# Reordering the router's chain in a fused two-layer transformer trunk: broadcast behind the logits, choice by token block, gathered rows by feature halves

## The reference

```
x = x + g_m * y                                   # attention's output
h = rms_norm(x, norm_ff[1]) * (1 + sc_f) + sh_f
logits = h @ router                               # 256 x 8
top_v, top_i = top_k(logits, 2); top_w = softmax(top_v)
for e in range(8):                                # w_in[e]: 1024 x 7168, w_out[e]: 3584 x 1024
    y += gates[:, e:e+1] * ((silu(a) * b) @ w_out[e])     # a, b = split(h @ w_in[e])
x = x + g_f * y; return rms_norm(x, final_norm)
```

## Time and profile before

| | |
|---|---|
| median of 3 runs | 1624.5 us (1624.39 to 1627.12) |
| profiled execution, its own time | 1623.05 us |
| its span (first to last instruction) | 1621.1 us |
| mean granted TensorE clock | 0.986 of 2.4 GHz |
| busy: TensorE, VectorE, ScalarE, GpSimd | 96%, 88%, 67%, 4% |
| read from memory | 499.28 MB, 309 GB/s over the span |

### The profile page before, as it was taken

One profiled execution on the slowest core, in us unless ns is written; L12 is line 12 of the kernel. 1 busy time (PEld: TensorE's weight loads), 2 busy tenths in 40 slices (PEclk: granted clock), 3 DMA queues, 4 the chain that ended last, 5 costly groups with the idle time before them and its releaser, 6 DMA issues.

```text
span 1621.1 us, 22979 instructions
## 1 busy us (share of the span) xinstructions
PE 1556.2 (96%) x7356; PEld 1292.5 (80%) x7356; DVE 1421.8 (88%) x1604; ACT 1085.2 (67%) x1224; POOL 59.7 (4%) x47
## 2 busy tenths in 40 slices
PE   5999998999989998999999999999999999999996
PEld 5788776888869777888888888888888888888884
DVE  6988999788878866989989989989989989999995
ACT  3454445344366647778878878878878778778774
POOL 0212200000000110000000000000000000000000
PEclk9999999999999999999999999999999999999998
DMA  9977777888845424999999999999999999999991
GB/s 333 346 251 268 269 263 247 291 287 306 318 179 208 156 79 152 394 363 349 372 366 341 370 371 336 367 376 337 371 373 333 365 376 341 367 375 344 363 378 76
DMA packets 235114, 500.91 MB, mean 309 GB/s; under 512 B 9744, under 2 KB 40640, under 8 KB 235072
## 3 DMA queue, kind: packets, MB, share of 16 engines
q1 hardware_dynamic: 233904, 500.29, 85.2%
q10 hardware_dynamic: 1168, 0.07, 0.0%
HBM read 499.28 MB, written 1.05 MB: 309 GB/s over the span
## 4 chain that ended last, share of the span: by engine, by line
PE 81%; DVE 9%; DMA 3%; issue 3%; ACT 2%; POOL 1%; SPq 0%; ACTq 0%; DVEq 0%; POOLq 0%
PE ps L500 24%; PE ps L502 24%; PE ps L501 24%; DMA ada<-in_ada_w 2%; DVE acc L1477 2%; DVE w_lo L1458 2%; PE ps L988 2%; PE ps L778 1%; PE ps L780 1%; PE ps L782 1%; DMA raw<-in_ret_w_in 1%; PE ps L1021 1%; PE ps L997 1%; PE ps L1022 0%; PE ps L998 0%
## 5 line engine op out<-in xcount | busy, mean ns | idle before, releaser
L1458 DVE TENSOR_TENSOR w_lo<-raw,w_hi 128x1024 fp32r<-128x1024 f32 x834 | 990.6, 1227 | 67.4 <-ACT w_hi L1088 55.3
L1088 ACT ACTIVATE w_hi<-raw 128x1024 fp32r<-128x1024 f32 x834 | 861.0, 1057 | 214.3 <-PE ps L502 188.3
L500 PE MATMUL ps<-w_hi,RA 128*128 128x512 f32 x1528 | 605.7, 396 | 9.9 <-DVE w_lo L1458 3.5
L502 PE MATMUL ps<-w_hi,RA 128*128 128x512 f32 x1528 | 596.5, 390 | 0.0
L501 PE MATMUL ps<-w_lo,RA 128*128 128x512 f32 x1528 | 595.8, 390 | 0.0
L500 PEld LDWEIGHTS ps<-w_hi,RA 128*128 128x128 f32 x1528 | 287.3, 188 | 69.2 <-DVE w_lo L1458 4.2
L502 PEld LDWEIGHTS ps<-w_hi,RA 128*128 128x128 f32 x1528 | 287.2, 188 | 61.1
L501 PEld LDWEIGHTS ps<-w_lo,RA 128*128 128x128 f32 x1528 | 287.7, 188 | 58.0 <-issue 0.7
L500 PE MATMUL ps<-w_hi,hT_hi 128*128 128x512 f32 x400 | 161.0, 402 | 6.4 <-issue 4.0
L502 PE MATMUL ps<-w_hi,hT_lo 128*128 128x512 f32 x400 | 158.3, 396 | 0.0
L501 PE MATMUL ps<-w_lo,hT_hi 128*128 128x512 f32 x400 | 158.0, 395 | 0.0
(11 more groups left out here) (249 smaller groups left out, 1042.1 us busy)
## 6 DMA issues: line engine op xcount, KB each, us to landing
raw<-in_moe_w_in SPq DMA_DIRECT2D x224, 1024.0 KB
raw<-in_moe_w_out SPq DMA_DIRECT2D x112, 1024.0 KB
ada<-in_ada_w SPq DMA_DIRECT2D x46, 1024.0 KB, 7.3
raw<-in_ff_w_in SPq DMA_DIRECT2D x44, 512.0 KB
raw<-in_ret_w_in SPq DMA_DIRECT2D x16, 1024.0 KB
raw<-in_ff_w_out SPq DMA_DIRECT2D x11, 1024.0 KB
raw<-in_ret_w_in SPq DMA_DIRECT2D x16, 512.0 KB
raw<-in_ret_w_out SPq DMA_DIRECT2D x8, 1024.0 KB
```

The lines of the kernel that those rows point to most:

```text
L500: pe.matmul(out, a_hi, b_hi, start=first, stop=False)
L502: return pe.matmul(out, a_lo, b_hi, start=False, stop=last)
L1088: act.activation(w_hi[:, cn % RING, cols], raw[:, cn % RAW, cols], ACT.Copy).then_inc(hi_done, 1)
L1458: v.tensor_tensor(w_lo[:, cn % RING, cols], raw[:, cn % RAW, cols], w_hi[:, cn % RING, cols].bitcast(f32), ALU.subtract).then_inc(lo_done, 1)
```

## The change

The gate's broadcast leaves its place between the second transposes and the second logits; its two matmuls go behind the logits and behind the counts, one each. The second block's sum of x is made in two column halves, each with its own semaphore count, and the transposes wait for each half. The choice is made by token block, and TensorE's first counts wait for block 0 alone; the subtraction for the softmax goes behind the choice. The gathered features are laid out over two PSUM banks so that each engine modulates two chunks of the first 512 features, then two of the second; `up` waits for each 512 features by itself. All calls of `turn_over` go.

```diff
-            def broadcast_gate(g, dg, bank):
+            def broadcast_gate(g, dg, bank, parts=range(2)):
                 pe.wait_ge(diag_ok, g + 1)
-                for n in range(2):
+                for n in parts:
                     last = pe.matmul(ps[:, bank + n, :], ones[:, :],
                                      dg[:, 4 * n:4 * n + 4, :].rearrange("p c q -> p (c q)"), start=True, stop=True)
-                last.then_inc(gbc_done, 1)
+                if 1 in parts:
+                    last.then_inc(gbc_done, 1)
...
             reduce_ada(2, 6)
-            turn_over(4, 20)
...
             def transpose_raw(b):
-                pe.wait_ge(x_ok, 5 + b)
                 for c in range(KC):
+                    if c % 4 == 0:
+                        pe.wait_ge(x_ok, 5 if b == 0 else 6 + c // 4)
...
             transpose_raw(1)
-            broadcast_gate(3, diag3, 2)
             route(1)
-            turn_over(0, 8)
+            broadcast_gate(3, diag3, 2, (0,))
 
             pe.wait_ge(sel_ok, 1)
             pe.matmul(ps[:, 5, 0:8], before[:, :], sel[:, 0, :], start=True, stop=True)
             pe.matmul(ps[:, 5, 8:16], ones[:, :], sel[:, 0, :], start=True, stop=False)
+            pe.wait_ge(sel_ok, 2)
             pe.matmul(ps[:, 5, 8:16], before[:, :], sel[:, 1, :], start=False, stop=True).then_inc(slot_done, 1)
             pe.matmul(ps[:, 1, 0:8], ones[:, :], sel[:, 0, :], start=True, stop=False)
             pe.matmul(ps[:, 1, 0:8], ones[:, :], sel[:, 1, :], start=False, stop=True).then_inc(cnt_done, 1)
+            broadcast_gate(3, diag3, 2, (1,))
...
-            def up(c, m, bank):
+            def up(c, m, bank, gathered=None):
                 for h in range(2):
+                    if gathered is not None:
+                        pe.wait_ge(hgl_ok, gathered + h + 1)
...
-                turn_over(0, 4)
                 transpose_gathered(NE * p)
-                turn_over(0, 14)
-                pe.wait_ge(hgl_ok, NB * NE * p + 2)
-                up(U_MOE, m0, 0)
+                up(U_MOE, m0, 0, 2 * NE * p)
...
             def gathered_high(ne):
                 act.wait_ge(hgT_done, ne + 1)
-                for c in range(4):
-                    ins = act.activation(hg32[:, c, :], ps[:, 6, c * P:(c + 1) * P], ACT.Identity,
-                                         bias=modc[:, FF1 + SH + c:FF1 + SH + c + 1], scale=scol[:, 4, c:c + 1])
-                ins.then_inc(hg32a_ok, 1)
-                act.wait_ge(hg32a_ok, ne + 1)
-                act.activation(hg_hi[:, 0:4, :], hg32[:, 0:4, :], ACT.Copy).then_inc(hgh_ok, 1)
-                act.wait_ge(hg32b_ok, ne + 1)
-                act.activation(hg_hi[:, 4:8, :], hg32[:, 4:8, :], ACT.Copy).then_inc(hgh_ok, 1)
+                for i in range(2):
+                    for c in range(4 * i, 4 * i + 2):
+                        col = c // 4 * S + c % 2 * P
+                        ins = act.activation(hg32[:, c, :], ps[:, 6, col:col + P], ACT.Identity,
+                                             bias=modc[:, FF1 + SH + c:FF1 + SH + c + 1], scale=scol[:, 4, c:c + 1])
+                    ins.then_inc(hg32a_ok, 1)
+                    act.wait_ge(hg32a_ok, 2 * ne + i + 1)
+                    act.wait_ge(hg32b_ok, 2 * ne + i + 1)
+                    act.activation(hg_hi[:, 4 * i:4 * i + 4, :], hg32[:, 4 * i:4 * i + 4, :],
+                                   ACT.Copy).then_inc(hgh_ok, 1)
...
+                if n == 2 and b == 1:
+                    for k in range(2):
+                        cols = slice(k * TW, (k + 1) * TW)
+                        v.tensor_tensor(x[:, b, cols], x[:, b, cols], tmp[:, b, cols], ALU.add).then_inc(x_ok, 1)
...
             for b in range(NB):
                 dve.wait_ge(rt_done, b + 1)
...
+                steps.link(v.scalar_tensor_tensor(logit[:, b, :], ps[:, 6 + b, 0:NE], stat[:, 6 + b:7 + b], sh_e, ALU.mult,
+                                                  ALU.add))
+                steps.link(v.max(mx[:, b, :], logit[:, b, :]))
+                steps.link(v.max_index(ridx[:, b, :], mx[:, b, :], logit[:, b, :]))
+                steps.link(v.tensor_copy(stat[:, 36 + 2 * b:38 + 2 * b], ridx[:, b, 0:2]))
                 for k2, oh in enumerate((oh1, oh2)):
                     ins = v.tensor_scalar(oh[:, b, :], slot_no[:, 0:NE], stat[:, 36 + 2 * b + k2:37 + 2 * b + k2], None,
                                           ALU.is_equal)
...
+                steps.link(ins)
+                v.tensor_tensor(sel[:, b, :], oh1[:, b, :], oh2[:, b, :], ALU.add).then_inc(sel_ok, 1)
+            v.tensor_tensor(stat[:, 32:34], mx[:, :, 1], mx[:, :, 0], ALU.subtract).then_inc(dm_ok, 1)
             normed_low(1)
```

More of the change, by code:

```diff
@@ L549, in transpose_x @@
                         last.then_inc(xT_done, 1)
-            def turn_over(bank, times):
-                for _ in range(times):
-                    pe.transpose(ps[:, bank, 0:P], ident[:, :], ident[:, :])
-            def broadcast_gate(g, dg, bank):
+            def broadcast_gate(g, dg, bank, parts=range(2)):
                 pe.wait_ge(diag_ok, g + 1)
-                for n in range(2):
+                for n in parts:
                     last = pe.matmul(ps[:, bank + n, :], ones[:, :],
                                      dg[:, 4 * n:4 * n + 4, :].rearrange("p c q -> p (c q)"), start=True, stop=True)
-                last.then_inc(gbc_done, 1)
+                if 1 in parts:
+                    last.then_inc(gbc_done, 1)
             pe.wait_ge(const_ok, 1)
@@ L1004, in transpose_gathered @@
                 for c in range(KC):
-                    last = pe.transpose(ps[:, 6 + c // 4, (c % 4) * P:(c % 4 + 1) * P], ht[:, c * P:(c + 1) * P],
-                                        ident[:, :])
+                    col = c // 4 * S + c % 2 * P
+                    last = pe.transpose(ps[:, 6 + c // 2 % 2, col:col + P], ht[:, c * P:(c + 1) * P], ident[:, :])
                 last.then_inc(hgT_done, 1)
@@ L1028, in step @@
                 pe.wait_ge(eg_ok, n)
-                up(c, me, 0)
+                up(c, me, 0, 2 * ne + 2 if j == ET else None)
                 if j == ET + 1:
@@ L1098, in root_mean_square @@
                 if 0 < n < 4:
-                    act.wait_ge(x_ok, NB * (n - 1) + b + 1)
+                    act.wait_ge(x_ok, NB * (n - 1) + b + 1 + (n == 3 and b == 1))
                 if n == 4 and b == 0:
@@ L1543, in add_gated @@
                 steps.link(ins)
-                v.tensor_tensor(x[:, b, :], x[:, b, :], tmp[:, b, :], ALU.add).then_inc(x_ok, 1)
+                if n == 2 and b == 1:
+                    for k in range(2):
+                        cols = slice(k * TW, (k + 1) * TW)
+                        v.tensor_tensor(x[:, b, cols], x[:, b, cols], tmp[:, b, cols], ALU.add).then_inc(x_ok, 1)
+                else:
+                    v.tensor_tensor(x[:, b, :], x[:, b, :], tmp[:, b, :], ALU.add).then_inc(x_ok, 1)
             dve.wait_ge(vecT_done, 1)
@@ L1866, in _ @@
                                           ALU.is_equal)
-            steps.link(ins)
-            v.tensor_tensor(sel, oh1, oh2, ALU.add).then_inc(sel_ok, 1)
+                steps.link(ins)
+                v.tensor_tensor(sel[:, b, :], oh1[:, b, :], oh2[:, b, :], ALU.add).then_inc(sel_ok, 1)
+            v.tensor_tensor(stat[:, 32:34], mx[:, :, 1], mx[:, :, 0], ALU.subtract).then_inc(dm_ok, 1)
             normed_low(1)
@@ L1911, in gathered_low @@
                 dve.wait_ge(hgT_done, ne + 1)
[L1912 to L1915, removed]
+                for i in range(2):
+                    for c in range(4 * i + 2, 4 * i + 4):
+                        col = c // 4 * S + c % 2 * P
+                        ins = v.tensor_scalar(hg32[:, c, :], ps[:, 7, col:col + P], scol[:, 4, c:c + 1],
+                                              modc[:, FF1 + SH + c:FF1 + SH + c + 1], ALU.mult, ALU.add)
+                    ins.then_inc(hg32b_ok, 1)
                 for i in range(2):
```

2 lines of the change are left out of this document (removed).

## The result

The changed kernel takes 1627.85 us (median of 20 runs, 1625.85 to 1631.54) against 1624.6 us of 20 runs of the kernel before: ratio 1.0022, 95% interval 1.0016 to 1.0028, about 3.6 us slower. The profiled execution of the changed kernel, the only one of this kernel whose trace is read here, was one of its longest, 1631.41 us with a span of 1629.7. So its times are read as distances inside a stage and not as places in the span.

What follows compares the result with a forecast made beforehand. TensorE, 81% of the chain and never idle in the expert loops, was taken as the bound, so only the first `up` could move: -1.0 -1.4 +0.4 +0 +0.5 = -1.5 us, from 1624.5 to 1623.0, range 1620.5 to 1626.3.

Steps and rivals of the forecast that it cites:

- part 1, the logits: Second block's logits in the router: start at 606.3 us instead of 608.57, end at 608.2.
- Part 2, ScalarE becomes the late one: Behind the late broadcast ScalarE needs 4.75 us; gathered rows' copy starts at 617.2 instead of 618.21, 1.0 us gained.
- register read: Rival, chance 0.10: ScalarE's read of the pass count isn't hidden and costs 1.2 us, giving 1624.2 us.
- drain beside a table load: ScalarE's table switch before the exponential: the skill's page gives 2.66 us with a drain; the prediction took none.
- Part 1, the choice by block: VectorE's choice in the router: 1.5 us per block, against 2.1 us for both; choice complete about 2.2 us earlier.
- VectorE's own work would decide: In the router's choice, VectorE's two blocks from 607.3 end at 610.3 us, later than the second logits allow.
- Part 3: Feature halves: `up` starts 2.2 us after the gathered rows are transposed instead of 3.63; saves 1.4 us, expert loops unaffected.
- Part 4, the dummies: Removing 46 dummy transposes costs through the clock: +0.4 us in transposes, 0 in first `up`, +0.5 at first tile.
- the worse of my two cases: Gathered rows' eight transposes run at the low clock, 1.93 instead of 1.09 us, +0.8 us at even chance.
- The first tile's copy: Retention's first tile without dummies: +0.2 us or +1.7 with a whole low stretch added; +0.5 taken.
- the clock that costs more than the chain gains: Rival, chance 0.15: low clock at retention's first tile and the first `up` makes the kernel +1.8 us slower, 1626.3 us.

Runs made afterwards that it cites:

- e9: Changed kernel with the first half of the broadcast made twice more, without a signal, ahead of the second logits; ratio 1.0008 to the kernel before.
- e4: Changed kernel with ScalarE making the weight quarter and the exponential before the gate copy; ratio 1.0008 to the kernel before.
- e7: Kernel before with the feature halves alone; ratio 0.9991 to the kernel before.
- e1: Kernel before with all 46 dummy transposes removed and nothing else changed; ratio 1.0016 to the kernel before.
- e2: Kernel before without the router chain's 26 dummy transposes, keeping the 20 ahead of the retention layer; ratio 1.0009 to the kernel before.
- e5: Changed kernel, no dummies, with both broadcast matmuls back between the second transposes and the second logits; ratio 1.0007 to the kernel before.
- e3: Changed kernel with all 46 dummy transposes put back, 8 of them behind the first half of the broadcast; ratio 1.0027 to the kernel before.
- e6: Changed kernel with the broadcast back in front of the second logits and all 46 dummy transposes back; ratio 0.9981 to the kernel before.

## Why the prediction was wrong

I forecast 1623.0 us, a gain of 1.5, and it became a loss of about 3.6, outside my range.

**What failed is part 1, the logits: "start 606.3 instead of 608.57, end 608.2"**, a duration of 1.85 us taken over unchanged. The start came out to the hundredth (4.73 us behind the first logits, 606.3 less 601.57), and the duration was 3.58. The row came from a stretch at the full clock. My own rows had the low stretch at 604.4 to 607.6, and the logits were moved into it. In the old order the broadcast ran there; the logits then found the clock at 2.4 GHz. Removed from its place, it left TensorE with eight transposes, waits and matmuls of 8 columns, and the clock didn't come back until the gather. Before the move, then, it was the broadcast that paid for the slow stretch. I weighed the clock for the broadcast, the transposes and `up`, but not for the logits and the counts. The logits took 1.73 us more; 0.6 of that VectorE would have needed anyway by my sum, so the choice was complete 1.1 us later than I had it (9.86 us behind the first logits, not 8.73). The counts took 2.0 us against my 0.7, since all five, and not three, stood behind the choice, queued behind the first broadcast half and at the low clock. The second half of the broadcast took 2.05 against 1.0 to 1.9. Together the broadcast's end is 14.05 us behind the first logits instead of the 10.4 to 11.3 that I summed. e9 confirms it: extra matmuls ahead of the logits make the kernel faster.

**Part 2, ScalarE becomes the late one: right, and the delay went through it whole.** Predicted 4.75 us from broadcast to copy, measured 4.80, no register read in between, so that rival falls. No drain beside a table load either: the exponential starts 0.01 us behind it, as the prediction's row had it against the Trainium skill ("ScalarE: Activation LUTs", What ACT_TABLE_LOAD costs). The copy stands 18.89 us behind the first logits; I had 15.6, and before it was 16.64. e4 prices the queue at 2.3 us by its ratio; 1.8 us of it are ScalarE's in the trace.

**Part 1, the choice by block**: 615.78 to 617.29 is 1.51 us, predicted 1.5, and block 0's is done during the logits. That VectorE's own work would decide was wrong: it waited 1.30 us for the logits.

**Part 3: right.** 2.37 us from the transposed rows to `up`, predicted 2.2; e7 gives 1.5 us, predicted 1.4. No wait in the loops.

**Part 4, the dummies: right in kind, mis-sized.** I took +0.9; e1 shows +2.6 us (0.0016, interval 1.1 to 3.9). The eight transposes ran low, 1.97 us, as in the worse of my two cases (in e1, e2, e4 and e5, also without dummies around them, they took 1.10). `up` and what follows it up to L988 lost 1.1 us more than before, where I took 0: this term was the mis-sized one. The first tile's copy was 1.46 us later in this trace where I took 0.5, but over all traces the difference is about 0.7, so that term isn't refuted (though I misread its row: the low stretch of before began some 0.4 us into the tile, not ahead of it). The Trainium skill's sentence that transposes don't count for the clock ("TensorE: Matmul & The Clock Gate", Part 4) doesn't agree with e1 and e2: both are slower without the dummies, with a low stretch of 6.8 us instead of 3.4 around the first `up`. But e3 shows that transposes don't always hold the clock either.

**The sum.** From the first logits to the transposes behind `up` the trace has 39.00 us and my terms make 34.1 (36.10 less 1.0 and 1.4, plus 0.4). Of the 4.9 between them 3.3 arise up to the gathered copy, 0.5 in the eight transposes, 0.1 in the halves and 1.1 in `up`. The gap between forecast and measurement is 5.1 us.

By the ratios: dummies +0.0016, feature halves -0.0009, sum by halves and choice by block -0.0010 (e6 to e7), the broadcast's move +0.0015 (changed to e5) sum to +0.0012; measured +0.0022. The intervals are 0.001 wide on each side, so this doesn't contradict, and it doesn't prove that the parts add up. Most of the missing 0.0010 is there if the dummies are priced in the new order (0.0026, e5 to e6) and not in the old one (0.0016): the parts seem to depend on one another, which the 0.0046 for the move with the dummies kept says more plainly. Of my rivals the one that came true is the clock that costs more than the chain gains (0.15), at another place than I gave it.

Open: the first logits stand at 601.57 us in the trace of before and at 607.43 in that of after, and over all traces between 601.3 and 607.4 without order (e4 and e9, without dummies, 601.42 and 601.32; e7, with them, 606.11). Read against each other at the same operations of ScalarE, the two traces part in three places, none of which the router's edits touch: 1.5 us at the first tile; 2.8 us more in the retention layer, by the operation at 197 us of the kernel before; and 1.6 us more between 267 and 290, where the changed kernel's trace has a second low stretch, 282.4 to 286.0, and the one of before has none. e4 and e9, without dummies too, have neither of the last two. So at least these two belong to the spread from run to run; what makes the one in the retention layer I didn't find.

## What to carry to other kernels

A duration taken from a trace holds for the clock it was measured at: before moving a short step, look at the granted clock of the place it moves into, and at what heavy work leaves that place. Moving work off the path can take away what brought the clock back, and a dummy costs its own time where the engine's next real work is nearly due (e3). When a signal is made later, follow every engine that waits for it in order: the 4.8 us that ScalarE needed from the gate copy to the gathered copy went into the chain whole, and moving the gate copy behind the exponential took 1.8 of them away. Where traces of one kernel differ by several us ahead of the place of interest, read distances, and look at more than one trace before calling a difference the edit's.

## What the runs showed of the hardware

Eight logits matmuls (16 weight loads of 128 columns with 8 moving ones) took 1.85 us at 2.4 GHz and 3.58 us at 1.2 GHz, with weight loads filling all of the 3.44 us looked at: such steps nearly double with the low clock, as the wide matmuls do (0.43 us apart against 0.23). The first block's logits, also at 2.4 GHz, took 1.93 us.

A low stretch isn't always as short as the four of the kernel before (3.2 to 3.4 us): behind 1.7 us of transposes, 0.88 us idle and the logits it went on for about 13.5 us, in e3 for 17 us with TensorE shown busy nearly throughout, and with 3 us of wide matmuls in the same place (e9, e6) the clock was back for the logits.

The column of the granted clock can miss a stretch. In e4, e5 and e9 it reads 1.00 from 34 to 60 us, while the first tile's matmuls stood 0.43 us apart up to about 48 us, as at the low clock; the spacing of the matmuls is the check.
